# Turning probabilities two groups at a time before two groups are multiplied with the values, with a fourth buffer for turned ones

## The reference, cut to what matters

```python
def dsa_block(q, iq, iw, qpos, k_all, v_all, ik_all, topk):      # group A: 8 heads, 2 kv heads
    ...                                                          # score, top-k of the keys per query
    s = jnp.einsum('bqngd,bqknd->bqngk', qg, k_sel).astype(jnp.float32) * (HEAD_DIM ** -0.5)
    s = jnp.where(valid[:, :, None, None, :], s, -jnp.inf)
    p = jax.nn.softmax(s, axis=-1).astype(v_sel.dtype)
    o = jnp.einsum('bqngk,bqknd->bqngd', p, v_sel)

def swa_prompt(b_q, b_k, b_v, sink):                             # group B: 4 heads, window of 3 chunks
    s = jnp.einsum('bcqngd,bcknd->bcngqk', qc, kband).astype(jnp.float32) * (HEAD_DIM ** -0.5)
    p = sink_softmax(s, sink).astype(vband.dtype)
    o = jnp.einsum('bcngqk,bcknd->bcqngd', p, vband)

def memory_attend(m_q, mk, mv):                                  # group M: 4 heads, 256 memory rows
    s = jnp.einsum('bqhd,bmhd->bhqm', m_q, mk).astype(jnp.float32) * (HEAD_DIM ** -0.5)
    p = jax.nn.softmax(s, axis=-1).astype(mv.dtype)
    o = jnp.einsum('bhqm,bmhd->bqhd', p, mv)

y = jnp.concatenate([o_a, o_b, o_m], axis=-1) * jax.nn.silu(gate)
x = x + jnp.einsum('btm,md->btd', y, w_out_l)
```

## Time and profile before

| | us |
|---|---|
| median of three executions | 1703.4 |
| the profiled execution | 1698.95 |
| its span | 1697.2 |
| PE busy | 1561.7 (92%) |
| DVE busy | 1028.4 (61%) |
| ACT busy | 660.1 (39%) |
| idle PE in the attention, by the trace, for copies of turned groups by ACT (L641) | 11.2 |

### The profile page before, as it was taken

One profiled execution on the slowest core, in us unless ns is written; L12 is line 12 of the kernel. 1 busy time (PEld: TensorE's weight loads), 2 busy tenths in 40 slices (PEclk: granted clock), 3 DMA queues, 4 the chain that ended last, 5 costly groups with the idle time before them and its releaser, 6 DMA issues. The chain is left out here.

```text
span 1697.2 us, 19595 instructions
## 1 busy us (share of the span) xinstructions
PE 1561.7 (92%) x6364; PEld 828.4 (49%) x6364; DVE 1028.4 (61%) x2685; ACT 660.1 (39%) x1628; POOL 118.8 (7%) x155
## 2 busy tenths in 40 slices
PE   2999999999889999999779999999997999999992
PEld 1544456666544444444444445566664444444451
DVE  0444526887667778767224453488766677777752
ACT  1223426775533323333112242477664333334332
POOL 0100013300000000000001001131000000000003
PEclk9999799999899999999679997999997999999976
DMA  7111310210411111010051004002004111111005
GB/s 270 53 40 33 132 45 1 84 54 39 173 40 37 38 38 38 1 38 19 24 185 50 24 22 146 25 1 112 40 38 162 38 38 38 38 38 38 20 1 232
DMA packets 80956, 105.22 MB, mean 62 GB/s; under 512 B 18864, under 2 KB 57488, under 8 KB 80784
## 3 DMA queue, kind: packets, MB, share of 16 engines
q1 hardware_dynamic: 80864, 104.04, 17.7%
HBM read 78.48 MB, written 29.97 MB: 64 GB/s over the span
## 5 line engine op out<-in xcount | busy, mean ns | idle before, releaser
L656 PE MATMUL score_ps<-w_slot,hT 128*128 128x512 f32 (+2 forms) x1024 | 388.6, 538 | 5.5 <-DMA w_slot<-in_w_in_dram 5.0
L656 PEld LDWEIGHTS score_ps<-w_slot,hT 128*128 128x128 f32 x1024 | 195.9, 194 | 186.3 <-issue 180.2
L1014 ACT ACTIVATE hT<-hT,neg_top 128x128 f32<-128x128 f32 (+8 forms) x144 | 118.1, 820 | 380.3 <-DVE neg_top L1263 380.1
L656 PE MATMUL score_ps<-w_slot,work 128*128 128x512 f32 x512 | 236.7, 617 | 0.5 <-ACT prob_bm L1027 0.5
L1158 DVE TENSOR_SCALAR_CACHE_REDUCE work<-bias,trial 128x384 f32<-128x384 f32 (+3 forms) x256 | 226.0, 883 | 6.9
L881 ACT ACTIVATE work<-bias,neg_trial 128x768 bf16<-128x768 f32 (+2 forms) x192 | 198.4, 1043 | 67.3 <-DVE neg_trial L1154 67.3
L786 PE MATMUL score_ps<-akT,query_mem 64*128 64x512 f32 (+4 forms) x448 | 194.7, 553 | 13.7 <-ACT prob_bm L1027 6.7
L656 PEld LDWEIGHTS score_ps<-w_slot,work 128*128 128x128 f32 x512 | 97.9, 196 | 124.8 <-issue 124.5
L1254 DVE CUSTOM_DVE_ANT_0 hT<-score_ps,bias 128x128 f32<-128x128 f32 (+8 forms) x144 | 115.7, 804 | 34.8 <-PE score_ps L786 33.9
L727 PE MATMUL score_ps<-hT,w_slot 128*128 128x352 f32 x448 | 135.2, 460 | 1.4 <-ACT gate_raw L1003 1.4
L786 PEld LDWEIGHTS score_ps<-akT,query_mem 64*128 64x128 f32 (+1 forms) x448 | 71.9, 185 | 114.0 <-issue 93.2
(11 more groups left out here) (174 smaller groups left out, 1777.1 us busy)
## 6 DMA issues: line engine op xcount, KB each, us to landing
gate_raw<-x_scratch SPq DMA_DIRECT2D x32, 512.0 KB, 3.7
w_slot<-in_w_in_dram SPq DMA_DIRECT2D x8, 2048.0 KB, 9.4
gate_scratch<-gate_raw SPq DMA_DIRECT2D x16, 528.0 KB, 2.7
w_slot<-in_w_out_dram SPq DMA_DIRECT2D x4, 2048.0 KB, 11.1
work<-gate_scratch SPq DMA_DIRECT2D x16, 512.0 KB, 4.7
x_scratch<-gate_raw SPq DMA_DIRECT2D x16, 512.0 KB, 2.6
hT<-x_scratch SPq DMA_DIRECT2D x8, 512.0 KB, 8.0
out_dram<-hT SPq DMA_DIRECT2D x8, 512.0 KB, 4.6
```

Source lines behind the costliest of these rows:

```text
L656: last = nc.tensor.matmul(out[:, 0:cols], lhs(k), w[:, k, 0:cols], start=(k == 0), stop=(k == KD - 1))
L1014: nc.scalar.activation(p, p, ACT.Exp, bias=neg_b[0:r, j:j + 1], scale=SM_SCALE, accum_out=sums[t % 2][0:r, cols]).then_inc(prob_done, 1)
```

## The change

The group of a `PT` step is no longer turned at once. It is held until a second group is there (or the last group of all is reached); then both are turned, one behind the other, and then the two groups turned before them are multiplied. Whatever the list lays between the two groups (QK and SCALE steps of a later item) now stands ahead of both. Four groups can be alive at once, so a fourth buffer is added; it is a tensor of its own, and the scratch space of dynamic DMAs is made smaller beside it. The instructions themselves, their number and their shapes are the same.

```diff
-    steps, late, waiting = [], [], []
+    steps, late, waiting, held = [], [], [], []
+    last_group = (len(ITEMS) - 1, len(groups_of(ITEMS[-1])) - 1)
...
-            steps.append(("PT", i, g))
-            if len(late) == 2:
-                steps += finish()
+
+
+            held.append(("PT", i, g))
+            if len(held) == 2 or (i, g) == last_group:
+                steps += held
+                while late:
+                    steps += finish()
+                late += [("PV",) + s[1:] for s in held]
+                held.clear()
             if g == 0 and waiting:
                 steps.append(waiting.pop())
 
             waiting += [s for s in scale if ITEMS[s[1]][1] != "A"]
             steps += [s for s in scale if ITEMS[s[1]][1] == "A"]
-            late.append(("PV", i, g))
...
-        prob_t = [work[:, 2112 + 512 * b:2624 + 512 * b] for b in range(3)]
+        prob_t = [work[:, 2112 + 512 * b:2624 + 512 * b] for b in range(3)] + [sb("prob_t3", [P, 512])[:, :]]
...
-                                                            prob_t[a % 3][0:w, r * m:r * (m + 1)],
+                                                            prob_t[a % 4][0:w, r * m:r * (m + 1)],
...
-                            if a >= 3:
-                                act.wait_ge(pv_done, a - 2)
-                            nc.scalar.copy(prob_t[a % 3][0:w, 0:n], bank.rearrange("p k n -> p (k n)")[0:w, 0:n]).then_inc(free, 1)
+                            if a >= 4:
+                                act.wait_ge(pv_done, a - 3)
+                            nc.scalar.copy(prob_t[a % 4][0:w, 0:n], bank.rearrange("p k n -> p (k n)")[0:w, 0:n]).then_inc(free, 1)
...
-    nc = _bacc.Bacc("TRN2", target_bir_lowering=False, num_devices=1)
+    nc = _bacc.Bacc("TRN2", target_bir_lowering=False, num_devices=1, dynamic_dma_scratch_size=1024)
```

8 lines of the change are left out of this document (4 added, 4 removed).

## The result

The changed kernel takes 1712.3 us (median of 20 runs) against 1699.0 us for the kernel before (median of 20 runs on the same chips): a ratio of 1.0079, 95% interval 1.0061 to 1.0097. The median of 1703.4 us from which the prediction started came from three runs and was 4 us too high.

A forecast was written before the change was run, and what follows sets the result against it. PE was taken to bound the second stretches, the chain over DVE and ACT to end the first ones last. Chain loss 8 us plus clock 14 us made 22 us on 1703.4, rounded to 1724 us, range 1697 to 1748.

The forecast's parts named there:

- 8 for this chain: Attention, both layers: first stretches' loss less gains of second stretches and tile 0, 4.0 us lost per layer, 8 in both.
- The price of a change of form: PE switching between turned blocks and products: 0.15 us per change, 126 fewer changes a layer, 38 us in both if PE-bound.
- Second stretches: PE work from OUT t 0's end to OUT t 1's start: fewer form changes and moved pairs gain 8.0 us per layer.
- First stretches of tiles 1 to 7: PE work from the previous tile's last OUT to OUT t 0: ACT's late copy makes them lose 13.0 us per layer.
- The distance of 6.6 us: From the M maximum's start to OUT's start, with ACT's copy behind four exponentials; before it was 3.65 to 5.6 us.
- Tile 0: The start of each layer's attention: put at 1 us gained per layer.
- The clock: New PE waits lower the granted clock in OUT at tiles 2, 4, 6 and 7: 7 us per layer, 14 in both.
- the third rival: The chain without the clock: PE's new waits come, but the granted clock falls no more often; 1711 us, chance 0.22.
- my own case: The late-copy chain plus more clock falls: 22 us slower, 1724 us, own range 1714 to 1738, chance 0.43.
- The list of what would show it: Trace signs: eight turned blocks in 1.0 us, PE idle 2 to 4 us for ACT's copy, MIX before OUT, OUT 8 to 9 us.
- Two of the signs of being wrong: In the trace: second stretches with new waits of over 1 us, and OUT at 7.1 us after long waits.
- the first rival: PE is the bound: saved form changes count and held copies come early enough; 1665 us, or 1684 with half, chance 0.10.

The follow-up runs named there:

- the third experiment: Changed kernel's planner limited to hold pairs in the first stretches only, order of before between OUT t 0 and OUT t 1; ratio 1.0169 to the kernel before.
- the ninth: Order of the kernel before with the fourth buffer, DVE copying both groups turned behind the memory scoring; ratio 0.989 to the kernel before.
- the tenth: Changed kernel with DVE copying only the first of the two groups turned behind each memory scoring; ratio 0.9944 to the kernel before.
- the twelfth experiment: Changed kernel with single groups at the end of the first stretches, pairs elsewhere, and DVE's two copies; ratio 0.9864 to the kernel before.
- the seventh: Changed kernel with pairs in both stretches, but only inside one item and never across OUT; ratio 0.9987 to the kernel before.
- the eighth: Pairs everywhere inside one item only, plus DVE copying the first group turned behind each memory scoring; ratio 0.9977 to the kernel before.
- fourth: Changed kernel with DVE instead of ACT copying both groups turned behind the memory scoring; ratio 0.989 to the kernel before.
- eleventh: Changed kernel with DVE copying both groups and the last A product ahead of the pair's turning; ratio 0.9822 to the kernel before, 1669.1 us.

## Why the prediction was right, step by step

**The sign and the mechanism were right, the sizes in part by luck.** The first stretches lose more than the second ones gain, and the loss is a copy behind the four memory exponentials. The sum of 22 us was made of 8 for this chain and 14 for the clock; measured they are some 10 and some 2.4 (the table above), so that the time lies in the range, but not for the reason of its larger part. The runs show this: taken away from ACT, the copies give 1.9% against the changed kernel (0.989 by 1.0079); where only one of the two is taken away, the distance stays at 6.6 to 7.0 us. How much of it the pairs cost the other way is the third experiment: 1.7% when they stand in the first stretches alone.

**The price of a change of form** was taken as 0.15 us. Two kernels have the same mean granted clock of 0.946, the ninth (order of before) and the tenth (changed order). Their pages give for the engines, in that order:

```profile
PE 1547.4 (92%) x6364; PEld 824.0 (49%) x6364; DVE 1037.4 (62%) x2703; ACT 652.4 (39%) x1610; POOL 118.6 (7%) x155
```

```profile
PE 1517.3 (90%) x6364; PEld 835.6 (50%) x6364; DVE 1035.8 (62%) x2699; ACT 653.8 (39%) x1614; POOL 118.9 (7%) x155
```

PE is busy for 1547.4 and 1517.3 us: 30.1 us for 2 x 126 changes, 0.12 us each. The 16.1 and 15.6 us less work at full clock of the table above give 0.12 to 0.13 us as well. Two groups of the same form side by side take 1.03 or 1.01 us for 1.18, so products gain as much as turned groups, which no row of before had shown. The Trainium skill, "TensorEngine Tiling (Array Packing)", section "Key Properties", says that a change of tiling mode drains TensorE; by that rule the trace agrees, with 0.12 us as the price here.

**Second stretches**: predicted minus 8.0 us a layer, measured minus 9.2. The terms inside were less good. A group that moves behind OUT takes its own changes of form with it, 0.58 + 0.59 = 1.17 us and not 0.86, so 4.7 us of the 7.1 that tiles 0, 2, 4 and 6 gained is the moved groups, more than my 3.4. Tiles 1 and 3 gained nothing together (new waits of 0.32 and 1.11 us), tile 5 1.0 us. Tile 7 gained 1.1 us where I had put a loss of 1.0: the new waits came (3.6 us against 0.8; that PE never waits in these stretches was not quite so), but the granted clock there was higher, 0.70 against 0.59.

**First stretches of tiles 1 to 7**: predicted plus 13.0 us, measured plus 15.1 and 16.3. The distance of 6.6 us was met at tiles 2, 4 and 7 (6.43, 6.53, 6.57), where the turned groups ran at full clock, and at tiles 1, 3 and 5 it was 7.78, where they did not. Tile 2 shows that this is the clock: behind the same wait of 2.11 us its distance was 6.43 in layer 0 and 7.78 in layer 1. The prediction adds 2.95 us for tile 7, but 6.6 - 3.89 is 2.7; by its own numbers this part is 12.8 and not 13.0.

**Tile 0**: predicted minus 1 us, measured 0.0 and minus 0.8. Its memory maximum, too, had the copy behind it: a distance of 7.78 instead of 5.34.

**The clock** is the step that failed in size. The term "4 x 1.7 = 6.8, call it 7 us per layer and 14 in both" was the largest of the sum. All 16 OUTs of a layer take 118.3 us before and 118.4 after. The fall did spread over OUTs, from tiles 3 and 5 to 1, 3, 4, 5 and 6 (at tile 1 the clock was low before as well, but from 505.5 to 512.3 us, ahead of its OUT, which took 7.13 us: the prediction misread that), but it begins earlier, in the wait or in the groups behind it, so that part of the low time passes while PE stands idle or turns, and OUT loses 0.5 to 0.9 us instead of 1.7. What it adds to the turned groups and products is some 1.2 us at tiles 1, 3 and 5 (7.78 against 6.5), 3 to 4 us a layer, which is about what the first stretches came out above their forecast. Against that stands a gain that the prediction did not have: in tile 7's second stretch and last OUT the clock was low for 13.7 us instead of 20.5. In all the lower clock cost some 2.4 us more in both layers, where the prediction had 14. With this term at nothing for the OUTs the sum is 8 us; measured were 13.3. By its size the result is thus nearer to the third rival, 1711 us, than to my own case, whose own range of 1714 to 1738 it misses by 2 us.

**The list of what would show it**: right were the pairs at 1.0 us, the copy directly behind the four exponentials with PE idle for it for 2.1 to 3.5 us at tiles 1, 2, 3, 5 and 6 (at tile 4 1.28 us, after 2.08 for a copy of DVE, and 0.96 at tile 7), MIX as the last thing before OUT, and the waits for ACT's copies (39.5 us against 13.0 in all). Wrong was "OUT of 8 to 9 us in most tiles": it was 7.1 to 8.0. Two of the signs of being wrong did come: second stretches with new waits of over 1 us (1.1 at tile 3, 3.6 instead of 0.8 at tile 7), and OUT at 7.1 us after a long wait (tile 2, 2.11 us, in both layers). The second is where the clock term failed. PE also stood idle less often right before OUT than I had said; at tile 6 the second product of the pair filled the time of MIX.

**What I had not seen at all** is that the kernel before paid for the same thing. Its waits of 1.67 us at tile 3 and the like the earlier trace rows are ACT's copies behind the exponentials as well, and taking them away is worth 1.1% by itself, with no pairs. I had read these rows as evidence against the first rival and not as time to be saved.

What stays open: pairs and single groups end at the same 0.989 with DVE's copies, though PE has 30 us less to do with pairs. In layer 0 the second stretches take 8.3 us less, and the first ones with tile 0 give back 4.9 and the OUTs 3.0 (1.7 of that in OUT 7 0, 8.80 us instead of 7.13); that the former is DVE's chain from head to head was argued from its 0.25 us of wait per maximum and not tried. Nor do the runs show what decides whether the clock falls behind a wait, on which hang the 24.6 and 29.1 us of the last tile's first stretch in the twelfth experiment.

## What to carry to other kernels

Before putting two like operations side by side, follow the copies that they make late: an engine's list is in order, and a short copy behind a long wait (here four exponentials that wait for a maximum) can stop PE for most of that wait (here 2.74 us at tile 6). Give such a copy to the engine whose list has only short work in front of it; here that was worth 1.1% in the old order and 1.9% in the new, which ended at the same time. Time saved on the busiest engine by itself says little: 28.6 us less work on PE came with 41.9 us more idle time, so read which wait ends last before counting what the work costs. The Trainium skill, "PSUM — Partial Sum Buffer", section "Engine vs sequencer instructions", says that the queues of ScalarE and VectorE are strict FIFO; the trace agrees, with a copy ready at 739.7 that ran at 745.16.

## What the runs showed of the hardware that was not expected

- The length of a wait alone does not say whether the granted clock falls behind it. In the kernel before, waits of 1.67, 1.71 and 1.38 us at tiles 3, 4 and 5 were followed by OUTs of 8.83, 7.13 and 8.27 us:

```profile
640.08 0.63 PE L641 MATMUL turn_ps<-ident,hT 128*128 128x128 f32 x4 [1.71 <-ACT work L1038]
```

  The same rows with the same wait went either way: at tile 7 of the twelfth experiment (1.94 us) with 7.13 us of OUT in layer 0 and 8.81 in layer 1; behind 2.06 us in the seventh (7.13, layer 0) and the eighth (9.13). A wait of 0.90 us (fourth and eleventh, tile 6) left OUT at 7.1, but 0.96 us at tile 7 of both, with a second one of 0.5 to 0.7 right before OUT, came with OUTs of 8.80 in both layers; in the changed kernel the same two waits (0.96 and 0.72) came with 7.11. What decides it is not shown here.
- The clock can fall in the wait itself. At tile 3 of the changed kernel PE waited from 587.75 to 591.26 us, and the granted clock was 0.50 from 589.65 on; the turned groups already ran at 0.91 to 0.99 us.
- A fall can cost more than the wait ahead of it. At tile 7 of the eighth experiment the granted clock was 0.59 for the 7 us behind a wait of 2.06 us, which is mostly the 1.2 GHz of its two levels, and 0.78 in OUT: four scorings took 3.62 us instead of 1.90, OUT 9.13 instead of 7.13. Between the two layers of the twelfth it made 4.5 us, with a wait of 1.94 us in either.
- Taking away 1.5 us of wait at tile 3 gave 3.2 us: the wait and 1.73 us of OUT.
